# Low parts of split weights written over their raw copies, and the freed buffers given to expert weights

## The reference, cut to what matters

```python
for layer in range(2):
    h = rmsnorm(x, g_mix[layer])
    u = h @ w_mix_in[layer]                       # (256, 1024) @ (1024, 3088)
    att, go, cv = attention(u), gla(u), short_conv(u)
    x = x + concat([att, go, cv]) @ w_mix_out[layer]     # (256, 1024) @ (1024, 1024)
    h = rmsnorm(x, g_ffn[layer])
    if layer == 0:
        f = (silu(h @ w1) * (h @ w3)) @ w2        # hidden width 2816
    else:
        f = sum(gate[e] * swiglu(h, w1[e], w3[e], w2[e]) for e in range(8))   # hidden width 3584
    x = x + f
out = rmsnorm(x, g_final)
```

## Time and profile before

| | us |
|---|---|
| median of 3 runs | 1305.41 |
| lowest and highest | 1304.89, 1305.57 |
| span of the profiled execution | 1300.1 |
| TensorE busy in that span | 1254.0 |
| DVE busy | 366.3 |
| ACT busy | 246.1 |
| POOL busy | 23.0 |

### The profile page before, as it was taken

How to read it: one execution, slowest core, us unless ns; L and a number is a source line. 1 busy time by engine, 2 the same in 40 slices (tenths; PEclk the granted TensorE clock), 3 DMA queues, 4 the chain that set the end, 5 groups by cost and what they waited for, 6 DMA issues and landing times.

```text
span 1300.1 us, 29767 instructions
## 1 busy us (share of the span) xinstructions
PE 1254.0 (96%) x13303; PEld 732.6 (56%) x13303; DVE 366.3 (28%) x484; ACT 246.1 (19%) x328; POOL 23.0 (2%) x38
## 2 busy tenths in 40 slices
PE   9999999999999999999999999999799999999775
PEld 6998888888989823543433644443243453354222
DVE  4777644444667520110010111011012001001002
ACT  5654544333573300000000000000000000000001
POOL 3000000000100000000000000000000000000000
PEclk9999999999999999999999999999999999999998
DMA  9842744423856899999999999999999999999995
GB/s 312 297 155 104 266 177 176 176 89 115 285 181 235 346 409 404 407 360 408 408 408 408 408 407 408 408 408 408 409 408 408 408 402 409 399 409 408 402 409 210
DMA packets 132102, 430.77 MB, mean 331 GB/s; under 512 B 12407, under 2 KB 18839, under 8 KB 131842
## 3 DMA queue, kind: packets, MB, share of 16 engines
q1 hardware_dynamic: 130354, 423.49, 83.9%
q0 software_dynamic: 1616, 5.33, 1.1%
HBM read 427.72 MB, written 2.11 MB: 331 GB/s over the span
## 4 chain that ended last, share of the span: by engine, by line
PE 86%; DMA 11%; SPq 1%; DVE 1%; ACT 1%; issue 0%; POOL 0%; POOLq 0%; DVEq 0%
PE psum L1901 34%; PE psum L1921 16%; PE psum L1422 9%; PE psum L1424 9%; PE psum L1423 9%; DMA ring<-in_moe_w 8%; DMA ring<-in_moe_w_end 2%; PE psum L1638 1%; PE psum L1875 1%; PE psum L1958 1%; PE psum L1850 1%; PE psum L1441 1%; SPq L494 0%; PE psum L1774 0%; PE psum L1597 0%; SPq L504 0%
## 5 line engine op out<-in xcount | busy, mean ns | idle before, releaser
L1901 PE MATMUL psum<-ring,xe 128*32 128x512 f32 (+1 forms) x5376 | 519.3, 541 | 19.9 <-DMA ring<-in_moe_w 14.9
L1901 PEld LDWEIGHTS psum<-ring,xe 128*32 128x32 f32 x5376 | 168.5, 110 | 350.7 <-issue 270.8
L1921 PE MATMUL psum<-ring,gT 128*32 128x256 f32 x4640 | 260.6, 381 | 11.1 <-DMA ring<-in_moe_w 11.0
L1921 PEld LDWEIGHTS psum<-ring,gT 128*32 128x32 f32 x4640 | 147.9, 110 | 127.5 <-issue 20.4
L1281 DVE TENSOR_TENSOR gate<-gate,psum 128x768 f32<-128x768 f32 (+3 forms) x32 | 24.6, 767 | 527.2 <-ACT gate L825 527.2
L920 DVE TENSOR_TENSOR wlo<-raw,whi 128x2048 fp32r<-128x2048 f32 (+1 forms) x66 | 145.3, 2229 | 58.7 <-ACT whi L651 58.4
L825 ACT ACTIVATE gate<-psum 128x768 f32<-128x768 f32 (+3 forms) x32 | 21.1, 661 | 614.2 <-PE psum L1901 614.2
L651 ACT CAST whi<-raw 128x2048 fp32r<-128x2048 f32 (+1 forms) x66 | 120.2, 1862 | 56.9 <-PE psum L1424 32.5
L1422 PE MATMUL psum<-whi,f_hi 128*128 128x512 f32 (+1 forms) x320 | 123.8, 387 | 1.1 <-DVE wlo L920 0.9
L1424 PE MATMUL psum<-whi,f_lo 128*128 128x512 f32 (+1 forms) x320 | 121.4, 379 | 0.0
L1423 PE MATMUL psum<-wlo,f_hi 128*128 128x512 f32 (+1 forms) x320 | 121.3, 379 | 0.0
(11 more groups left out here) (249 smaller groups left out, 795.7 us busy)
## 6 DMA issues: line engine op xcount, KB each, us to landing
ring<-in_moe_w SPq DMA_DIRECT2D x608, 512.0 KB, 14.4
raw<-in_ffn_w SPq DMA_DIRECT2D x33, 1024.0 KB, 5.6
ring<-in_moe_w_end SPq DMA_DIRECT2D x64, 512.0 KB, 14.7
raw<-in_w_mix_in SPq DMA_DIRECT2D x21, 1024.0 KB, 7.5
raw<-in_w_mix_out SPq DMA_DIRECT2D x8, 1024.0 KB, 5.3
raw<-in_w_mix_in SPq DMA_DIRECT2D x4, 544.0 KB, 6.0
x<-in_x SPq DMA_DIRECT2D x2, 512.0 KB, 4.3
raw<-in_w_mix_in SPq DMA_DIRECT2D x2, 512.0 KB, 6.4
```

The source lines that it names most:

```text
L1901: ins = mm(banks(j, n)[o:o + 32, g, 0:2 * q].rearrange("p (i b c) -> p i b c", i=2, c=64), rows_[:, k * CAP + 32 * g:k * CAP + 32 * (g + 1 ...
L1921: ins = mm(bank[bk][32 * q:32 * (q + 1), at_:at_ + 256], gT[j % 2][:, a:a + 32], w[:, o:o + 256], start=j == 0 and n == 0 and at_ == 0, st ...
```

## The change

1. The three fixed raw buffers are no longer raw buffers; their place stays free (`early_at`, `EARLY_FIXED`). `raw[i]` is now the same memory as `wlo[i]`, for all six slots, in the mixers too. DVE subtracts in place.
2. A block has one slot for its raw, high and low parts (`slot_of`): n % 6 up to block 50, and from there a fixed order of its own. SP loads block n when TensorE has used the block before it in that slot (`block_used`, by `slot_free` and `used_after`, which knows the four blocks at the end of the dense layer that are used out of order). ACT waits only for the landing.
3. In each full dense chunk, split n+5 stands behind gT of (c, 0) instead of ahead of it, on ACT and DVE.
4. Ring buffers 1 to 3 are the freed place, with no wait on splits, and the loads of ring blocks 0 to 3 stand in SP's order behind block 49 and ahead of the second mixer's loads. The loads from ring block 4 on stay behind them with the waits that they had.
5. The wait of SP for `mix_ready` 4 in the first dense chunk goes, since no raw buffer lies in the arena any more.

```diff
-def raw_plan():
...
+def slot_of(n):
+
+    if n <= BASE[1]:
+        return n % SLOTS
+    return (BASE[1] + (3, 4, 1, 2, 5, 0)[(n - BASE[1] - 1) % SLOTS]) % SLOTS
+
+
+def uses_of(n):
+
+    return sum(slot_of(i) == slot_of(n) for i in range(n + 1))
+
+
+def used_after(n):
+
+    late = {BASE[1] - 5: 2, BASE[1] - 4: 2, BASE[1] - 3: -2, BASE[1] - 2: -2}
+    return n + 1 + late.get(n, 0)
+
+
+def slot_free(n):
+
+    before = [i for i in range(n) if slot_of(i) == slot_of(n)]
+    return used_after(before[-1]) if before else None
...
-        raw_at = at[0]
-        raw = [place(f"raw{i}", BLOCK) for i in range(RAW_FIXED)]
+        early_at = at[0]
+        at[0] += 4 * BLOCK * EARLY_FIXED
         w_at = [at[0], at[0] + SLOTS * 4 * BLOCK]
         whi = [place(f"whi{i}", BLOCK, F32R) for i in range(SLOTS)]
         wlo = [place(f"wlo{i}", BLOCK, F32R) for i in range(SLOTS)]
+        raw = [place(f"raw{i}", BLOCK, offset=w_at[1] + 4 * BLOCK * i) for i in range(SLOTS)]
...
-        pairs_at = [w_at[i] + 8192 * ((MOE0 - SLOTS + n) % SLOTS) for n in range(SLOTS) for i in range(2)]
-        ring_at = [spare_at] + [raw_at + 8192 * i for i in range(RAW_FIXED)]
+        pairs_at = [w_at[i] + 8192 * slot_of(MOE0 - SLOTS + n) for n in range(SLOTS) for i in range(2)]
+        ring_at = [spare_at] + [early_at + 8192 * i for i in range(EARLY_FIXED)]
...
             def fill(n, src, rows, cols, turn=0, per=0, uses=0):
...
-                until = None if before is None else sp.lower_val(per * turn + before + 1)
+                until = None if free is None else sp.lower_val(per * turn + free)
                 load = sp.dma_start(dst, src)
                 if until is not None:
-                    load.wait_op(lo_ready, until, "sem-ge")
+                    load.wait_op(block_used, until, "sem-ge")
...
-                        if c == 0 and i == 1 and k == 1:
-                            sp.wait_ge(mix_ready, 4)
...
-                if 1 <= f < EARLY:
-                    sp.wait_ge(lo_ready, MOE0 - RAW_FIXED + f)
-                elif EARLY <= f < EARLY + 6:
+                if EARLY <= f < EARLY + 6:
...
-                load_up(PER_SWEEP * sweep, 0, 0, 0)
+                load_up(PER_SWEEP * sweep, 0, 0, 0, range(0 if sweep else EARLY, KD))
...
             fill(n + 2, ktiles(ffn_w2[0][DENSE_FULL * FC:, :]), 2, D)
+            load_up(0, 0, 0, 0, range(EARLY))
             mixer(1)
...
             def split(n, turn=0, per=0):
...
-                act.wait_ge(raw_full[s], 16 * (per // SLOTS) * turn + 16 * raw_use[n])
-                if n >= SLOTS:
-                    late = 2 if n in (BASE[1] + 1, BASE[1] + 2) else 0
-                    act.wait_ge(block_used, per * turn + n - SLOTS + 1 + late)
-                nc.scalar.copy(whi[w][:, 0:size], raw[s][:, 0:size]).then_inc(hi_ready, 1)
+                act.wait_ge(raw_full[w], 16 * (per // SLOTS) * turn + 16 * uses_of(n))
+                nc.scalar.copy(whi[w][:, 0:size], raw[w][:, 0:size]).then_inc(hi_ready, 1)
...
                 if c < DENSE_FULL:
-                    for k in range(2):
-                        split(n + 4 + k, turn, 6)
+                    split(n + 4, turn, 6)
                     d_gT(c, 0, turn)
+                    split(n + 5, turn, 6)
                     for k in range(4 if c < DENSE_FULL - 1 else 2):
                         split(n + 6 + k, turn, 6)
```

More of the change, by code:

```diff
@@ L84 @@
 SLOTS = 6
-RAW_FIXED = 3
+EARLY_FIXED = 3
 K_ID, K_IOTA, K_DOWN = 0, P, 2 * P
@@ L147, in trunk @@
           g_cols_in, consts_in, masks_in, onehot_in, out):
-    raw_slot, raw_use, raw_before = raw_plan()
     ctx = ExitStack()
@@ L226, in trunk @@
         setup_router = place("setup_router", 64, offset=base["bias0"] + 5 * 2048 + 256)
-        at[0] = ffn_arena
-        raw += [place(f"raw{i}", BLOCK) for i in range(RAW_FIXED, SLOTS)]
+        at[0] = ffn_arena + 3 * 4 * BLOCK
         gate_out = [place(f"gate_out{i}", FC) for i in range(2)]
@@ L424, in fill @@
             def fill(n, src, rows, cols, turn=0, per=0, uses=0):
-                s = raw_slot[n]
-                before = raw_before[n]
+                s = slot_of(n)
+                free = slot_free(n)
                 dst = raw[s][:, 0:rows * cols].rearrange("p (k c) -> p k c", k=rows)
-                until = None if before is None else sp.lower_val(per * turn + before + 1)
+                until = None if free is None else sp.lower_val(per * turn + free)
                 load = sp.dma_start(dst, src)
                 if until is not None:
-                    load.wait_op(lo_ready, until, "sem-ge")
+                    load.wait_op(block_used, until, "sem-ge")
                 load.then_inc(raw_full[s], 16)
@@ L443, in mixer @@
                     if l == 0 and i == 0:
-                        sp.dma_start(raw[raw_slot[0]][:, 0:4 * nc_].rearrange("p (k c) -> p k c", k=4),
+                        sp.dma_start(raw[0][:, 0:4 * nc_].rearrange("p (k c) -> p k c", k=4),
                                      w[:, 0:4, c:c + nc_]).then_inc(raw_first, 16)
-                        sp.dma_start(raw[raw_slot[0]][:, 4 * nc_:8 * nc_].rearrange("p (k c) -> p k c", k=4),
-                                     w[:, 4:8, c:c + nc_]).then_inc(raw_full[raw_slot[0]], 16)
+                        sp.dma_start(raw[0][:, 4 * nc_:8 * nc_].rearrange("p (k c) -> p k c", k=4),
+                                     w[:, 4:8, c:c + nc_]).then_inc(raw_full[0], 16)
                         continue
@@ L863, in _ @@
             act.wait_ge(raw_first, 16)
-            nc.scalar.copy(whi[0][:, 0:1024], raw[raw_slot[0]][:, 0:1024]).then_inc(hi_first, 1)
+            nc.scalar.copy(whi[0][:, 0:1024], raw[0][:, 0:1024]).then_inc(hi_first, 1)
             turn_hi(0, 0)
-            act.wait_ge(raw_full[raw_slot[0]], 16)
-            nc.scalar.copy(whi[0][:, 1024:2048], raw[raw_slot[0]][:, 1024:2048]).then_inc(hi_ready, 1)
+            act.wait_ge(raw_full[0], 16)
+            nc.scalar.copy(whi[0][:, 1024:2048], raw[0][:, 1024:2048]).then_inc(hi_ready, 1)
             turn_hi(0, 1)
@@ L915, in split @@
             def split(n, turn=0, per=0):
-                s, w = raw_slot[n], n % SLOTS
+                w = slot_of(n)
                 size = block_size(n)
                 dve.wait_ge(hi_ready, per * turn + n + 1)
-                nc.vector.tensor_tensor(wlo[w][:, 0:size], raw[s][:, 0:size], whi[w][:, 0:size].bitcast(F32),
+                nc.vector.tensor_tensor(wlo[w][:, 0:size], raw[w][:, 0:size], whi[w][:, 0:size].bitcast(F32),
                                         ALU.subtract).then_inc(lo_ready, 1)
@@ L1367, in _ @@
                 norm_row(0, t)
-            first = raw[raw_slot[0]]
+            first = raw[0]
             dve.wait_ge(hi_first, 1)
@@ L1426, in weights @@
             def weights(n, k, cols, c0, c1):
-                w = n % SLOTS
+                w = slot_of(n)
                 return (whi[w][:, k * cols + c0:k * cols + c1], wlo[w][:, k * cols + c0:k * cols + c1])
@@ L1797, in dense_up @@
                 if c < DENSE_FULL:
-                    blocks = [((n + k) % SLOTS, 4, 6 * turn + n + k + 1) for k in range(2)]
+                    blocks = [(slot_of(n + k), 4, 6 * turn + n + k + 1) for k in range(2)]
                     width = FC
@@ L1801, in dense_up @@
                     n = DENSE0 + 6 * c + i
-                    blocks = [(n % SLOTS, 8, n + 1)]
+                    blocks = [(slot_of(n), 8, n + 1)]
                     width = HALF
@@ L1811, in dense_down @@
                 if c < DENSE_FULL:
-                    blocks = [((n + k) % SLOTS, 6 * turn + n + k + 1) for k in range(2)]
+                    blocks = [(slot_of(n + k), 6 * turn + n + k + 1) for k in range(2)]
                 else:
                     n = DENSE0 + 6 * c + 2
-                    blocks = [(n % SLOTS, n + 1)]
+                    blocks = [(slot_of(n), n + 1)]
                 down(4 + 2 * t, gT_hi[t], gT_lo[t], blocks, c == 0, c == DENSE_FULL, gT_ready,
```

2 lines of the change are left out of this document (1 added, 1 removed).

## The result

| | before | after |
|---|---|---|
| median, us | 1304.89 | 1310.14 |
| lowest and highest of 7 runs each | 1302.73, 1307.16 | 1307.47, 1312.2 |
| ratio to before (95% interval) | | 1.0040 (1.0028 to 1.0051) |
| span of the profiled execution | 1300.1 | 1310.2 |

The change costs 5.3 us, where 1.6 us were forecast. Of the profiled execution of after the device time is known too, 1311.97 us, 1.8 us over its span. If the same 1.8 us hold before, its profiled execution took some 1302 us and was one of the quick ones. So the 10.1 us between the two spans are more than the kernels differ by, and the first thing to do is to part what the change did from what one execution did.

What follows compares the result with a forecast made beforehand. TensorE was taken to bound the first third and the DMA engines the end. Terms 0 + 0 + 0.8 + 0.6 + 0.2 + 0 + 0 = 1.6 us on 1305.4 gave 1307.0 us; 8-in-10 range 1304.8 to 1310.0.

Steps and rivals of the forecast that it cites:

- B: End of the dense layer, block 50: its load queues behind the eight ring transfers; cost 0.6 us, bounds 0 and 1.5.
- 0.9 to the end: Last part of the 5.1 us assumed for a load's landing: 1.6 to the start, 2.6 for bytes, 0.9 to the end.
- C: Middle of both mixers, blocks 15, 16, 65, 66: splits wait for landings; 0.1 us a mixer, 0.2 in all, bounds 0 and 1.0.
- It fits by 0.1 us: Mixers' middle: the convolution's product was put at 93.74 us, and TensorE wants it at 93.82.
- A: End of the first mixer, block 19: additions to x wait behind its split; cost 0.8 us, bounds 0.5 and 1.2.
- D: Dense chunks, split n+9: fits by 0.9 us, four times; cost 0, bounds 0 and 4.8 us.
- the first slow rival: Dense turns: TensorE waits at each of four for late landings, 1309 to 1311.8 us; over 1308.0 had chance 0.28.
- The in-place subtraction: DVE's split written onto one of its operands: nothing in the trace says this costs; 0 us.
- The start: Loads 3, 4 and 5 asked for at 8 us; TensorE's 0.9 us wait hangs on a cast, not a transfer: 0 us.
- The preload: Ring blocks 0 to 3 asked for ahead of the second mixer's loads: gain 0 us, at most 10.3 us.
- the fast rival: Experts' start: the four early ring blocks relieve it, down to 1296.7 us; a time under 1302.8 had chance 0.11.
- The later arrival: At the experts: a later arrival of TensorE goes through both parts of their loading one to one.

Runs made afterwards that it cites:

- the experiment with two blocks: The changed kernel with only ring blocks 0 and 1 asked for early, 2 and 3 behind the second mixer; one run, 1302.58 us.
- the second profile: The changed kernel profiled and timed once more, unaltered: 1310.78 us, ratio 1.0060 to the kernel before.

## Why the prediction was wrong

**The size, at B.** The mechanism was right: load 50 queued behind the ring, a cast that waits, gT_hi and gT_lo behind it. The landing was put at 307.9, or 309.6 with the 1.7 us by which this execution was later; it was at 310.83. The bytes went nearly as forecast. Counted from 293 us, load 49 and the ring (5.24 MB) were through at about 306.0 us, where 305.8 was due, and block 50's bytes followed at some 350 GB/s until 308.75 us, where 308.7 was due. By then all but 0.07 MB had moved. The step that failed is the last, the "0.9 to the end": that remainder came at 127 GB/s and less for another us, and the landing was 2.1 us behind 308.75. The rows of after, and then that of block 50 in the kernel before, where the rate fell at 298.25 us and the load landed 0.85 us later, at 299.1:

```profile
308.00:309.00 1.00, 1.00 (x11) 1.00 (x10) 0.52 (x1) 0.00 (x0) 0.00 (x0) 1.00 0.91 286
309.00:310.00 1.00, 1.00 (x11) 1.00 (x10) 0.00 (x0) 0.00 (x0) 0.00 (x0) 1.00 0.52 71
```
```profile
298.00:299.00 1.00, 1.00 (x10) 1.00 (x10) 0.00 (x0) 0.00 (x0) 0.00 (x0) 1.00 0.28 96
```

Block 51 was asked for only at 308.7 us, so it did not take the bandwidth; why the end was slow behind a queue and not alone is not shown. The 1.2 us that the landing was later than forecast are the difference between B's 0.6 and the 1.8 us measured (1.7 to 2.0 in four other executions). In an execution where the clock falls behind the wait it is 3.6. The range named for B ended at 1.5 and had no term for the clock. By the Trainium skill, "DMA: Bandwidth & Descriptors", section "Queues, rings and completion order", each engine consumes the descriptors of its ring in order; the experiment with two blocks agrees, 5.2 us for 2.10 MB.

**The size, at C.** In mixer 1 it cost 1.4 to 1.6 us and not 0.1. The second of two loads asked for 1.4 us apart was given 6.2 us; in after it took 7.0 us in mixer 0 and 8.24 us in mixer 1, where the rate had fallen by 399 us and the landing came at 400.8: a slow end again. Over the profiles with the splits unmoved, the stretch grows by what this landing takes over some 6.6 us: +0.02 at 6.4 us, +0.03 at 6.6, +0.42 at 7.0, +1.06 at 7.7, +1.38 at 8.0, +1.62 at 8.24. So the chain on ACT and DVE had some 0.3 us more room than the forecast gave it, and the landing was the term that was wrong. Why it is longer in mixer 1 each time (7.7 to 8.24 us against 6.4 to 7.0) is not shown.

"It fits by 0.1 us" was read as a cost of 0.1, although the two mixers' landings had never been measured in this order. A fit that close needs the later landing as its central value. The bound given, 0.5 us a mixer, was also too small.

**Right.** A: 0.72 to 0.76 us against 0.8, in part by luck: the row of h made the transposes only 0.55 us late, and the other 0.2 us are the four transposes themselves, 0.67 us instead of 0.45, which the forecast hadn't. By the estimate from the Trainium skill, "DMA: Bandwidth & Descriptors", section "Anatomy of one DMA", 4.4 us for such a load, it would have been 0.2; the landing was 4.95. That section's figure is for transfers issued from GpSimd, and these are issued from SP. D: 0.0, all turns 16.99 us apart as before, so the first slow rival falls. The in-place subtraction: 0. The start: its +0.6 in after is less than the +1.1 of before run again, so no cost shows. The preload: 0, with the engines idle at 404 to 406, 408 to 410 and 432 to 434 us, as argued from the earlier trace rows; the fast rival falls. The later arrival passed one to one through the experts, 796.95 us against 796.93.

**The base.** The sum was added to a median of 1305.41 us with a profiled execution 5.3 us under it. After's own profiled run lies 1.8 us over its span, and the kernel before run again has a span of 1304.9 at a time of 1306.86. So the first profile was a quick execution, with 3.4 us of low clock behind the router where the second had 10.2, and the 5.3 us were no constant of the kernel. This moved no term, but it hid that a few microseconds come and go here by the clock.

In all: 3.95 us of waits by the second profile, where 1.6 were forecast, and 1 to 3 us in the timed runs whose place isn't shown, of which the clocks on record account for up to 1.8 as an estimate. The measured median, 1310.14, lies just outside the range's end of 1310.0, and the forecast of no change was wrong: it is slower.

## What to carry to other kernels

Bytes put ahead of a load that is needed soon delay it by all of them: here 4 MB asked for early were worth nothing and cost 1.7 us or more, while the same 4 MB asked for in or behind the second mixer, or half of them in the change's place, cost nothing. When a wait on an in-order engine turns from "slot free" to "landed", look at what stands behind it in that engine's program, and move the instruction that waits behind work that is ready; on the engine that only follows, leave the order alone. A margin of 0.1 us in such a chain is a cost of the landing's spread, and must be priced with the slowest landing of its kind. The last bytes of a load can take longer behind a queue than alone (2.1 us against 0.85 here), so a landing isn't its bytes at full rate plus a constant.

## What the hardware showed that was not expected

- After a wait of 1.8 us TensorE had a clock of 0.57 over 4 us in one execution (1.7 us lost); with the same wait of 1.4 to 1.7 us it stayed at 1.00 in four others.
- Behind the router's mask, where TensorE waits 0.4 us among short matmuls, it ran at 1.2 GHz for 3.4 to 13.7 us, differing between kernels and between two executions of one (3.4 and 10.2 us for before). Two more filler matmuls made the kernel 0.2% faster than it was, more than any form of the change did.
- A 1 MB load asked for 1.4 us behind another landed after 6.2 to 8.2 us, where the one ahead of it took 4.8 to 5.5; the end of it came slowly, in mixer 1 86 GB/s from 398 to 400 us and 4 GB/s in the two after.
